# Down projection: 13 of 44 pairs of k tiles by seven block products in place of eight, with a ring of eight loaded chunks

## The reference, cut to what matters

```python
h = rms_norm(x, norm1_w)
x = x + mixer(h, ...)                      # w_in, an mLSTM part, an attention part, w_out
h = rms_norm(x, norm2_w)
x = x + (silu(h @ w_gate) * (h @ w_up)) @ w_down     # 2048 -> 5632 -> 2048
```

## Time and profile before

| what | value |
|---|---|
| median of three runs | 1122.85 us (1122.55 to 1123.35) |
| the profiled execution's own time | 1125.04 us |
| its span, first to last instruction | 1123.2 us |
| PE busy | 1113.3 us (99%), 5020 matmuls |
| DVE busy | 734.6 us (65%) |
| ACT busy | 576.8 us (51%) |
| loads and stores | 212.46 MB, mean 189 GB/s |

### The profile page before, as it was taken

The page is one execution under the profiler, slowest core; times in us unless marked ns, Lnnn a source line. Parts: engine busy times, 40 slices in busy tenths (PEclk is TensorE's granted clock), DMA queues, the critical chain, the costliest instruction groups (busy, mean ns, idle before and its releaser), DMA issues.

```text
span 1123.2 us, 14985 instructions
## 1 busy us (share of the span) xinstructions
PE 1113.3 (99%) x5020; PEld 922.0 (82%) x5020; DVE 734.6 (65%) x876; ACT 576.8 (51%) x718; POOL 4.5 (0%) x20
## 2 busy tenths in 40 slices
PE   8999999999999999999999999999999999999998
PEld 6888887888888888888888888888888888888886
DVE  5566546764565566788787788788788644454443
ACT  7566466754545455446455455555555443343341
POOL 1000000000000000000000000000000000000000
PEclk8999999999999999999999999999999999999999
DMA  9555544564465646466566565565565756656554
GB/s 345 184 165 191 172 147 132 185 205 154 146 197 172 202 164 211 150 201 211 181 205 205 187 205 201 175 221 179 181 220 168 223 189 195 195 190 197 194 188 131
DMA packets 59796, 212.46 MB, mean 189 GB/s; under 512 B 6752, under 2 KB 6752, under 8 KB 59760
## 3 DMA queue, kind: packets, MB, share of 16 engines
q1 hardware_dynamic: 59552, 211.84, 57.1%
q10 hardware_dynamic: 144, 0.05, 0.0%
q0 software_dynamic: 64, 0.07, 0.0%
HBM read 209.83 MB, written 2.10 MB: 189 GB/s over the span
## 4 chain that ended last, share of the span: by engine, by line
PE 98%; DMA 1%; DVE 1%; ACT 0%; SPq 0%; issue 0%; ACTq 0%
PE acc L431 15%; PE acc L434 15%; PE acc L433 15%; PE acc L655 11%; PE acc L653 11%; PE acc L654 11%; PE aux L434 4%; PE aux L433 4%; PE aux L431 4%; PE aux L445 2%; PE aux L654 2%; PE aux L653 2%; PE aux L655 2%; DMA w_raw<-in_weights 1%; PE aux L495 0%; DVE res L1450 0%
## 5 line engine op out<-in xcount | busy, mean ns | idle before, releaser
L1060 DVE TENSOR_TENSOR w_lo<-w_raw,w_hi 128x1024 fp32r<-128x1024 f32 x231 | 280.8, 1223 | 241.1 <-ACT w_hi L750 119.6
L1393 DVE TENSOR_TENSOR w_lo<-w_raw,w_hi 128x1024 fp32r<-128x1024 f32 (+1 forms) x200 | 227.4, 1167 | 50.6 <-ACT w_hi L1008 23.6
L653 PE MATMUL acc<-w_lo,act_hi 128*128 128x512 f32 x520 | 203.2, 391 | 0.0
L655 PE MATMUL acc<-w_hi,act_hi 128*128 128x512 f32 x520 | 202.5, 389 | 0.0
L654 PE MATMUL acc<-w_hi,act_lo 128*128 128x512 f32 x520 | 202.3, 389 | 0.0
L750 ACT ACTIVATE w_hi<-w_raw 128x1024 fp32r<-128x1024 f32 x143 | 149.2, 1056 | 82.0 <-PE acc L434 73.9
L431 PE MATMUL acc<-w_lo,act_hi 128*128 128x512 f32 x448 | 179.1, 400 | 3.3 <-DVE w_lo L1060 3.3
L434 PE MATMUL acc<-w_hi,act_hi 128*128 128x512 f32 x448 | 175.7, 392 | 0.0
L433 PE MATMUL acc<-w_hi,act_lo 128*128 128x512 f32 x448 | 175.6, 392 | 0.0
L1011 ACT ACTIVATE w_hi<-w_raw 128x1024 fp32r<-128x1024 f32 x120 | 125.5, 1056 | 55.6 <-PE acc L655 32.2
L1032 ACT ACTIVATE w_hi<-w_raw 128x1024 fp32r<-128x1024 f32 x80 | 84.9, 1061 | 132.2 <-PE aux L434 132.2
(11 more groups left out here) (250 smaller groups left out, 1274.4 us busy)
## 6 DMA issues: line engine op xcount, KB each, us to landing
w_raw<-in_weights SPq DMA_DIRECT2D x391, 512.0 KB, 4.2
res<-in_x SPq DMA_DIRECT2D x4, 512.0 KB, 10.8
out<-res SPq DMA_DIRECT2D x8, 256.0 KB, 3.8
xt<-in_x_turned SPq DMA_DIRECT2D x3, 512.0 KB, 9.4
xt<-in_x_turned SPq DMA_DIRECT2D x2, 256.0 KB, 4.3
w_raw<-in_weights SPq DMA_DIRECT2D x2, 256.0 KB, 3.8
w_if<-in_gate_w POOLq DMA_DIRECT2D x1, 64.0 KB, 6.7
par<-in_params ACTq DMA_DIRECT2D x1, 47.0 KB, 3.6
```

Source lines behind the costliest of these rows:

```text
L653: pe.matmul(bank[:], hi, w_lo[:, slot, cols], start=start, stop=False)
L655: return pe.matmul(bank[:], hi, w_hi[:, slot, cols], start=False, stop=stop)
L1060: dve.tensor_tensor(w_lo[:, slot, :], w_raw[:, slot, :], w_hi[:, slot, :].bitcast(F32), ALU.subtract).then_inc(lo_done, 1)
L1393: dve.tensor_tensor(w_lo[:, c % SPLIT, cols], w_raw[:, slot, cols], w_hi[:, c % SPLIT, cols].bitcast(F32), ALU.subtract).then_inc(lo_done, 1)
```

## The change

Down: a plan written out ahead (`plan`, `PLAN`) lists the steps of all stages. In pass 0 five pairs of k tiles (from k = 18, 22, 26, 30, 34) and in pass 1 eight (from 6, 10, ... 34) become pairs of seven block products; the other 62 k tiles stay plain. DVE makes the sums of the hidden activations in four groups during pass 0, at steps 5, 9, 13 and 17 (`hidden_full`, `hidden_sums`, `hidden_sums_lo`; ACT makes their high halves). They lie where the normalised activations `act_hi` and `act_lo` were. A pair's products of their own (q1, q5, q6, q7) gather over a pass in the four banks that the other pass uses. `down_products` adds them to the residual in eight DVE instructions a pass, in the fourth and fifth step after the pass's last pair. PE waits for them before pass 1. The first pair of pass 1 waits for `output(0)`.

The ring `w_raw` has 8 slots for 4, and SP's loads beyond the eighth wait for the last use of the chunk eight before. The loops over slices and over down are written out on all engines. The slices' six evacuations use `stage` and `gated`, not a buffer of their own, and four of them now stand behind step 18 and two behind step 19. The next slice's first step waits on PE for `pre_ready` in place of `gate_act`. The two small loads move from POOL's queue to ACT's, behind chunk 1. With `SLICE_ORDER` as it stands a slice has the same order and the same two pairs as before, so the branches for `N_PAIRS == 3` do nothing.

```diff
-RAW = 4
+RAW = 8
+SLICE_ORDER = "gggggPguuPuuuu"
+DOWN_PAIRS = ((18, 22, 26, 30, 34), (6, 10, 14, 18, 22, 26, 30, 34))
+SUM_BLOCKS = (slice(4, 6), slice(6, 8), slice(3, 9, 5), slice(1, 3))
+SUM_AT = (5, 9, 13, 17)
...
+            for n in range(RAW, CHUNKS):
+                sp.wait_ge(lo_done, LAST_USE[n - RAW] + 1)
+                load(slice(n, n + 1), n % RAW)
...
-            pool.dma_start(w_if[:], gate_w).then_inc(wif_landed, 16)
-            pool.dma_start(bias_if[:], gate_bias).then_inc(bias_landed, 16)
...
+            def down_pair(p, n, k):
+                banks = [[acc[0], aux[2], acc[1]], [acc[2], aux[0], acc[3]]][p]
+                q1, q5, q7, q6 = [[acc[2], acc[3], aux[0], aux[1]], [acc[0], acc[1], aux[2], aux[3]]][p]
+                begin, end = k == DOWN_PAIRS[p][0], k == DOWN_PAIRS[p][-1]
+                if p == 0:
+                    pe.wait_ge(hid_lo_done, 2 * FF_SLICES)
+                    pe.wait_ge(down_e_lo, sum_place(k)[0] + 1)
+                else:
+                    pe.wait_ge(out_ready, 4)
+                    pe.wait_ge(down_e_lo, len(SUM_AT))
+                pe.wait_ge(lo_done, n + 1)
+                three(q1, *hidden_tile(k, 0), n % SPLIT, 0, begin, end).then_inc(chunk_used, 1)
+                pe.wait_ge(lo_done, n + 2)
+                three(banks[0], *hidden_tile(k + 1, 0), (n + 1) % SPLIT, 0, False, False)
+                three(banks[1], *hidden_sum(E3, k), (n + 1) % SPLIT, 1, False, False).then_inc(chunk_used, 1)
+                pe.wait_ge(lo_done, n + 3)
+                three(q5, *hidden_sum(E5, k), (n + 2) % SPLIT, 0, begin, end)
+                three(q7, *hidden_sum(E7, k), (n + 2) % SPLIT, 1, begin, end).then_inc(chunk_used, 1)
+                pe.wait_ge(lo_done, n + 4)
+                three(banks[2], *hidden_tile(k + 1, 1), (n + 3) % SPLIT, 0, False, False)
+                three(q6, *hidden_sum(E6, k), (n + 3) % SPLIT, 1, begin, end).then_inc(chunk_used, 1)
...
+                if n == 1:
+                    act.dma_start(w_if[:], gate_w).then_inc(wif_landed, 16)
+                    act.dma_start(bias_if[:], gate_bias).then_inc(bias_landed, 16)
...
+            def hidden_full(g):
+                if g:
+                    dve.wait_ge(down_e_lo, g)
+                parts = [h[:].bitcast(F32).rearrange("p (m f) s -> p m (f s)", f=4)[:, SUM_BLOCKS[g], NG:CH]
+                         for h in (hid_hi, hid_lo)]
+                dve.wait_ge(hid_lo_done, 2 * FF_SLICES - 2)
+                dve.tensor_tensor(scaled[:], parts[0], parts[1], ALU.add).then_inc(full_ready, 1)
...
+            def hidden_sums_lo(g):
+                dve.wait_ge(down_e_hi, g + 1)
+                dve.tensor_tensor(down_lo[:, 8 * P * g:8 * P * (g + 1)], gated[:].rearrange("p a n -> p (a n)"),
+                                  down_hi[:, 8 * P * g:8 * P * (g + 1)].bitcast(F32),
+                                  ALU.subtract).then_inc(down_e_lo, 1)
+
+            def down_products(p, part):
+                q5, q7, q6 = [[acc[3], aux[0], aux[1]], [acc[1], aux[2], aux[3]]][p]
+                q1 = [acc[2], acc[0]][p]
+                o = 8 * p
+                of = [[res[:, t, CH * p + NG * j:CH * p + NG * (j + 1)] for j in range(2)] for t in range(TT)]
+                if part == 0:
+                    dve.wait_ge(down_q1, p + 1)
+                    dve.tensor_tensor(stage[:, 0, :], q6[:], gated[:, 0, :], ALU.subtract).then_inc(down_step, 1)
+                    dve.tensor_tensor(of[0][0], of[0][0], q1[:], ALU.add).then_inc(down_step, 1)
+                    dve.wait_ge(down_step, o + 1)
+                    dve.tensor_tensor(stage[:, 1, :], q7[:], stage[:, 0, :], ALU.subtract).then_inc(down_step, 1)
+                    dve.tensor_tensor(gated[:, 1, :], q5[:], stage[:, 0, :], ALU.add).then_inc(down_step, 1)
+                else:
+                    dve.wait_ge(down_step, o + 4)
+                    dve.tensor_tensor(of[1][0], of[1][0], stage[:, 1, :], ALU.add).then_inc(down_step, 1)
+                    dve.tensor_tensor(of[0][1], of[0][1], gated[:, 1, :], ALU.add).then_inc(down_step, 1)
+                    dve.tensor_tensor(scaled[:, 0, :], gated[:, 1, :], q7[:], ALU.subtract).then_inc(down_step, 1)
+                    dve.wait_ge(down_step, o + 7)
+                    dve.tensor_tensor(of[1][1], of[1][1], scaled[:, 0, :], ALU.add).then_inc(down_step, 1)
```

More of the change, by code:

```diff
@@ L20 @@
 import math
+from collections import namedtuple
 from contextlib import ExitStack
@@ L70 @@
 CHUNKS = DOWN0 + 2 * KF
[L74 to L83, removed]
-E7, E5, E6, E3 = range(4)
-def step_raw(c):
-    return c if c < 5 else c - 2 if c < 12 else c - 4
+Step = namedtuple("Step", "kind index load part pair")
+SLICE_ORDER = "gggggPguuPuuuu"
@@ new lines, with sum_place, plan, add_pair @@
+HALF = SLICE_ORDER.count("g")
+N_PAIRS = SLICE_ORDER.count("P")
+PAIR_K = [12, 14, 10][:N_PAIRS]
+DOWN_PAIRS = ((18, 22, 26, 30, 34), (6, 10, 14, 18, 22, 26, 30, 34))
+SUM_BLOCKS = (slice(4, 6), slice(6, 8), slice(3, 9, 5), slice(1, 3))
+SUM_AT = (5, 9, 13, 17)
+E7, E5, E6, E3 = range(4)
+def sum_place(k):
+    m = k // 4
+    g = next(g for g in range(4) if m in range(*SUM_BLOCKS[g].indices(KF // 4)))
+    return g, list(range(*SUM_BLOCKS[g].indices(KF // 4))).index(m)
+def plan():
+    steps = [Step("one", n, n, 0, 0) for n in range(FF0 + FF_CHUNKS)]
+    load, pair, starts = FF0 + FF_CHUNKS, 0, []
+    def add_pair(index):
+        nonlocal load, pair
+        for part in range(4):
+            steps.append(Step("pair", index, load, part, pair))
+        load, pair = load + 2, pair + 1
+    for i in range(1, FF_SLICES):
+        starts.append(len(steps))
+        count = {"g": 0, "u": 0, "P": 0}
+        for kind in SLICE_ORDER:
+            if kind == "P":
+                add_pair(count["P"])
+            else:
+                steps.append(Step(kind, count[kind], load, 0, 0))
+                load += 1
+            count[kind] += 1
+    for p in range(2):
+        starts.append(len(steps))
+        k = 0
+        while k < KF:
+            if k in DOWN_PAIRS[p]:
+                add_pair(k)
+                k += 2
+            else:
+                steps.append(Step("one", k, load, 0, 0))
+                load, k = load + 1, k + 1
+    return steps, starts
@@ new lines @@
+PLAN, STARTS = plan()
+SLICE_START = [FF0] + STARTS[:FF_SLICES - 1]
+DOWN_START = STARTS[FF_SLICES - 1:]
+STEPS = SLICE_START[2] - SLICE_START[1]
+LAST_USE = {st.load + (st.part == 3): n for n, st in enumerate(PLAN) if st.kind != "pair" or st.part >= 2}
+PAIR_END = max(c for c in range(STEPS) if PLAN[SLICE_START[1] + c].kind == "pair")
+EVAC_AT = 18
+DOWN_PAIR_END = [max([n for n in range(DOWN_START[p], len(PLAN)) if PLAN[n].kind == "pair"
+                      and (p or n < DOWN_START[1])], default=0) for p in range(2)]
@@ L356, in _ @@
                     sp.dma_start(xt[:, xt_parts[n], :], x_turned[:, xt_parts[n], :]).then_inc(xt_landed[n], 16)
[L357 to L360, removed]
+                if n >= 4:
+                    c = slice(NG * (n - 4), NG * (n - 3))
+                    sp.dma_start(res[:, :, c], x_t[:, :, c]).then_inc(x_landed[n - 4], 16)
+                    sp.wait_ge(lo_done, n - 3)
                 load(slice(n, n + 1), n % RAW)
[L362 to L373, removed]
+            for n in range(RAW, CHUNKS):
+                sp.wait_ge(lo_done, LAST_USE[n - RAW] + 1)
+                load(slice(n, n + 1), n % RAW)
             for j in range(8):
@@ L661, in summed @@
             def summed(e, j):
+                if j == 2:
+                    return third_hi[:, P * e:P * (e + 1)], third_lo[:, P * e:P * (e + 1)]
                 cols = slice(2 * P * e + P * j, 2 * P * e + P * (j + 1))
                 return sum_hi[:, cols], sum_lo[:, cols]
[L665 to L680, removed]
@@ L682, in ff_slice, with ff_pair @@
[L682 to L695 removed]
+            def ff_pair(i, n, j):
+                q1, q5, q7, q6 = aux[2], aux[3], aux[0], aux[1]
+                k, begin, end = PAIR_K[j], j == 0, j == N_PAIRS - 1
+                pe.wait_ge(lo_done, n + 1)
+                three(q1, *tile(k, 0), n % SPLIT, 0, begin, end).then_inc(chunk_used, 1)
+                pe.wait_ge(lo_done, n + 2)
+                three(acc[0], *tile(k + 1, 0), (n + 1) % SPLIT, 0, False, end)
+                three(acc[2], *summed(E3, j), (n + 1) % SPLIT, 1, begin, False).then_inc(chunk_used, 1)
+                pe.wait_ge(lo_done, n + 3)
+                if begin:
+                    pe.wait_ge(hid_lo_done, 2 * i)
+                three(q5, *summed(E5, j), (n + 2) % SPLIT, 0, begin, end)
+                three(q7, *summed(E7, j), (n + 2) % SPLIT, 1, begin, end).then_inc(chunk_used, 1)
+                pe.wait_ge(lo_done, n + 4)
+                three(acc[1], *tile(k + 1, 1), (n + 3) % SPLIT, 0, False, end)
+                three(q6, *summed(E6, j), (n + 3) % SPLIT, 1, begin, end).then_inc(chunk_used, 1)
@@ new lines, in ff_slice @@
+            def ff_slice(i):
```

(48 more changed lines are left out.)

289 lines of the change are left out of this document (174 added, 115 removed).

## The result

The changed kernel takes 1112.43 us (median of four, 1112.18 to 1113.06) against 1122.70 us for the kernel before: 10.27 us less, ratio 0.9908 (0.9891 to 0.9925). The forecast was 1114.0 us with a range from 1112.6. The direction and 8.84 of the 10.27 us were as forecast.

The account below looks back on a forecast made before the run. The prediction took PE, busy 99%, as the bound, so the number of matmuls counts. Only the 39 saved matmuls counted, all other terms 0: 1122.85 - 8.84 = 1114.0 us, range 1112.6 to 1117.4 us.

Parts of the forecast that it names:

- What it removes: Down: thirteen pairs take 21 matmuls for 24, 39 fewer; at 226.7 ns each, 8.84 us less.
- What it adds on DVE: Down: four k tiles cost DVE about 9.4 us against PE's 10.2; about 0.9 us spare at the fourth part, no wait.
- The sums of the activations: Pass 0: four groups, 4.1 us of DVE each, hidden; cost 0, smallest margin 0.5 us at the first pair, bound 2.4.
- Products: Down: eight additions to the residual a pass, 5.4 us of DVE, done before PE needs them; cost 0.
- PE's queue: Down's pairs: six semaphore waits where two plain steps have two; cost 0, bound 2.9 us over 13 pairs.
- slices: Ten slices: same matmuls and order, evacuations moved by one or two instructions, looser start wait; length unchanged, 0.
- The ring: Down's weight loads: eight slots let loads go four chunks sooner; down asks for 206 GB/s; cost 0.
- The start: Kernel start: small loads on ACT delay chunk 2 by under 1.5 us, hidden; chunk 1's wait may shrink 0.2; taken as 0.
- The rival of the clock: Kernel start: slow-clock stretch may go or come again, 3.4 us either way, 1110.6 or 1117.4 us; chance 0.03 each.
- Sum. Only -8.84 us: Whole kernel: only the saved matmuls count, from the median 1122.85 to 1114.0 us.
- Writing the loops out takes branches away ... so I take 0: Slices: unrolling removes branches that could stall, but none held PE up in 453 to 878 us; gain 0.
- the tail: the four last additions remain as they are: Kernel end after pass 1: the products' additions add nothing to the tail; cost 0.

## Why the prediction was right, and where it was wrong

- **What it removes: right.** 39 matmuls at 226.7 ns, 8.84 us; measured against the same kernel without pairs, 8.86 us. The 8.4 us that the prediction took from the Trainium skill (TensorE: Matmul & The Clock Gate, "Back-to-back issue gap") are 0.4 us short, and the prediction left out what the section says around it: the formula is for an isolated matmul, and for a stream the section states about 131 ns at 512 columns. By that 39 matmuls would be 5.1 us, an estimate; the trace's 226.7 ns agree with neither figure.
- **What it adds on DVE: right.** The steady state of pass 1, DVE, ACT and PE of the changed kernel:

```profile
1025.99 1.22 DVE L1143 TENSOR_TENSOR w_lo<-w_raw,w_hi 128x1024 fp32r<-128x1024 f32 x1
1027.24 0.69 DVE L1158 TENSOR_TENSOR w_raw<-w_raw 128x512 f32<-128x512 f32 x1
1027.97 0.69 DVE L1160 TENSOR_TENSOR w_raw<-w_raw 128x512 f32<-128x512 f32 x1
1028.58 1.22 DVE L1143 TENSOR_TENSOR w_lo<-w_raw,w_hi 128x1024 fp32r<-128x1024 f32 x1
1030.92 4.10 DVE L1143 TENSOR_TENSOR w_lo<-w_raw,w_hi 128x1024 fp32r<-128x1024 f32 x4 [1.11 <-ACT w_hi L845]
...
1029.83 3.10 ACT L845 ACTIVATE w_hi<-w_raw 128x1024 fp32r<-128x1024 f32 x3 [1.66 <-PE aux L483]
...
1032.97 0.39 PE L702 MATMUL acc<-w_lo,hid_hi 128*128 128x512 f32 x1
```

The four splittings from 1030.92 on begin with the fourth part's; it ends at 1032.15, and PE begins that part at 1032.97. The spare is 0.8 us, for 0.9 named in the prediction (its own layout, 9.1 for 10.2 us, gives 1.1), and DVE idles 1.11 us a period for the 0.8 us that the sum left. The prediction's example of neighbours that overlap shows none: 1.25 us from start to start is more than the 1.22 us that the splitting takes. The sum does not rest on it.

- **The sums of the activations: right at 0, the margin sized too small.** In the first pair of pass 0 DVE does the fourth part at 926.88, 0.31 us behind the last group's low halves of 925.35, and PE begins it at 928.93:

```profile
925.35 1.22 DVE L1547 TENSOR_TENSOR act_lo<-gated,act_hi 128x1024 fp32r<-128x1024 f32 x1
926.88 4.10 DVE L1143 TENSOR_TENSOR w_lo<-w_raw,w_hi 128x1024 fp32r<-128x1024 f32 x4 [0.31 <-ACT w_hi L845]
...
928.93 0.39 PE L702 MATMUL acc<-w_lo,hid_hi 128*128 128x512 f32 x1
```

It is ready at 928.1, 0.8 us ahead, where 0.5 was named (the prediction's own 9.5 for 10.2 us gives 0.7). The wait of up to 2.4 us, which the range allowed for, did not come.

- **Products, PE's queue, slices: right**, all at 0; no new wait of PE, and the slices as long as before. (The prediction counts three waits of PE in the kernel before; the earlier trace rows has four, two of them in its first row. The 5.4 us are right.)
- **The ring: right at 0 for the change as it stands.** It is what lets the pairs keep their gain: with four slots 5.8 of the 8.9 us are lost.
- **The start: right at 0.** The queue of the small loads is worth nothing. The rival of the clock was weighed on one execution. That execution lay 2.2 us above the median of its kernel, and the slow stretch goes with that: the variants of before with slow last stores, whose start ran at 1.00, have spans of 1120.7 to 1121.2 us for 1123.2 us, and medians equal to before's. So the stretch costs 2.0 to 2.5 us, not the 3.4 us of the prediction. The prediction noted the 2.2 us and did not explain them. They mean that the stretch was already missing from the median, so there was nothing to gain.
- **The failed step: "Sum. Only -8.84 us", through "Writing the loops out takes branches away ... so I take 0" and "the tail: the four last additions remain as they are".** The tail's additions and issues did remain, to 0.01 us, but the last stores land 1.2 us sooner in the trace when PE's loop is written out (1.3 us by the medians for that edit alone; 1.4 us for all of the change but the pairs). I looked for the loops' price only where the branches are, and gave the written-out program no bound on the gain side. The range reached 1.4 us below the forecast, for the start and the spread of runs. That nearly covered the missing term by luck, and the last 0.2 us are little more than the median of the kernel before, which came out at 1122.70 us in place of 1122.85. The term of 1.4 us is the error. How the loop slows the stores stays open.
- **The rule on branches.** The Trainium skill (Runtime: NRT & Kernel Launch, "Instruction fetch mechanics") prefers written-out code because a taken branch can stall. It has the sign, but the gain is not where it puts it: the stretch of 436.14 us through the slices is as long with PE's loop as without.

## What to carry to other kernels

When PE is fed without a gap, a saving of matmuls is worth their number times the start-to-start interval, to a few hundredths of a microsecond, until the feeding engine's period reaches PE's. Lay one period out by hand with the durations of the trace and name the margin before trusting it. Saved matmuls shorten the time in which loads and splittings must arrive, so look at the ring together with the pairs. When a profiled execution lies more than the spread above its median, explain the difference before a term rests on it. Give a written-out program a bound on both sides, its end included.

## What was not expected of the hardware

A loop on PE that ended 240 us earlier goes with a slower pace of the last stores, and of those alone: packets of 2 KB in 0.16 us against 0.084 us, 257 and 259 GB/s against 300 and 303 over two microseconds, 1.2 us at the end of the span and 1.3 to 1.5 us in the medians (1121.35 and 1121.18 us against 1122.7). Loops on SP, ACT and DVE do nothing of the kind. The mechanism is open.
